# The low part of each MLP weight chunk: an accumulating DMA on a negated copy in place of a subtraction on DVE

## The reference, cut to what matters

```
h = rmsnorm(x, g)            # the first block adds shift and scale
y = square(relu(h @ W1)) @ W2    # W1: 1024 x 4096, W2: 4096 x 1024
x = x + y                    # the first block: x + gate * y
```

## Time and profile before

| | |
|---|---|
| time, median of 3 | 1957.42 us (1956.87 to 1958.24) |
| the profiled execution's own time | 1959.16 us |
| its span | 1957.3 us |
| PE busy | 1903.8 us |
| DVE busy | 966.7 us |
| ACT busy | 751.3 us |
| POOL busy | 76.7 us |
| matmuls | 8624 |

### The profile page before, as it was taken

The page is one execution under the profiler, slowest core; times in us unless marked ns, Lnnn a source line. Parts: engine busy times, 40 slices in busy tenths (PEclk is TensorE's granted clock), DMA queues, the critical chain, the costliest instruction groups (busy, mean ns, idle before and its releaser), DMA issues.

```text
span 1957.3 us, 21184 instructions
## 1 busy us (share of the span) xinstructions
PE 1903.8 (97%) x8624; PEld 1529.1 (78%) x8624; DVE 966.7 (49%) x1391; ACT 751.3 (38%) x1080; POOL 76.7 (4%) x94
## 2 busy tenths in 40 slices
PE   3999999989999999999999999999999999999999
PEld 2777668868888888877788888888877778888887
DVE  7367643554444346554554344445644554344443
ACT  4344443343323244356734232234445534233231
POOL 5100000010000000001100000000001000000000
PEclk9999999989999999999999999999999999999999
DMA  7445533313232223200122232322221122222222
GB/s 255 157 145 183 170 121 113 124 63 101 95 99 95 100 95 113 98 33 33 44 97 94 89 103 91 104 90 97 97 87 43 65 86 97 97 97 97 97 97 76
DMA packets 55121, 197.66 MB, mean 101 GB/s; under 512 B 6400, under 2 KB 6656, under 8 KB 55024
## 3 DMA queue, kind: packets, MB, share of 16 engines
q1 hardware_dynamic: 52272, 188.24, 28.2%
q0 software_dynamic: 2320, 7.31, 1.3%
q10 hardware_dynamic: 432, 0.74, 0.1%
HBM read 194.13 MB, written 2.14 MB: 100 GB/s over the span
## 4 chain that ended last, share of the span: by engine, by line
PE 93%; DVE 4%; ACT 2%; issue 0%; DMA 0%; POOL 0%; DVEq 0%; ACTq 0%
PE ps L252 26%; PE ps L254 25%; PE ps L253 25%; PE ps L288 2%; PE ps L290 2%; PE ps L289 2%; DVE RAW L1222 1%; PE ps L373 1%; PE ps L425 1%; PE ps L584 1%; PE ps L672 1%; DVE WL L1214 1%; PE ps L571 1%; PE ps L602 1%; PE ps L359 1%; PE ps L412 1%
## 5 line engine op out<-in xcount | busy, mean ns | idle before, releaser
L252 PE MATMUL ps<-R0h,WH 128*128 128x512 f32 x1200 | 471.6, 393 | 21.4 <-POOL R0l L1791 18.9
L1214 DVE TENSOR_TENSOR WL<-RAW,WH 128x1024 fp32r<-128x1024 f32 x303 | 372.3, 1233 | 241.0 <-ACT WH L769 237.5
L769 ACT ACTIVATE WH<-RAW 128x1024 fp32r<-128x1024 f32 x303 | 317.2, 1051 | 394.0 <-PE ps L254 339.5
L254 PE MATMUL ps<-R0h,WL 128*128 128x512 f32 x1200 | 468.2, 390 | 0.0
L253 PE MATMUL ps<-R0l,WH 128*128 128x512 f32 x1200 | 468.1, 390 | 0.0
L252 PE MATMUL ps<-R1h,WH 128*128 128x512 f32 x1064 | 420.8, 396 | 7.8 <-POOL R1l L1819 2.8
L253 PE MATMUL ps<-R1l,WH 128*128 128x512 f32 x1064 | 416.8, 392 | 0.0
L254 PE MATMUL ps<-R1h,WL 128*128 128x512 f32 x1064 | 416.7, 392 | 0.0
L252 PEld LDWEIGHTS ps<-R0h,WH 128*128 128x128 f32 x1200 | 225.9, 188 | 76.8 <-issue 16.5
L254 PEld LDWEIGHTS ps<-R0h,WL 128*128 128x128 f32 x1200 | 225.8, 188 | 47.4
L253 PEld LDWEIGHTS ps<-R0l,WH 128*128 128x128 f32 x1200 | 225.9, 188 | 46.1
(11 more groups left out here) (266 smaller groups left out, 1471.0 us busy)
## 6 DMA issues: line engine op xcount, KB each, us to landing
RAW<-in_W SPq DMA_DIRECT2D x351, 512.0 KB, 3.2
XT<-in_X SPq DMA_DIRECT2D x4, 512.0 KB, 7.7
ARENA<-bias_scratch POOLq DMA_DIRECT2D x8, 256.0 KB, 3.3
XT<-in_X POOLq DMA_DIRECT2D x8, 256.0 KB, 3.6
out_x<-XT SPq DMA_DIRECT2D x8, 256.0 KB, 2.0
ARENA<-bias_scratch POOLq DMA_DIRECT2D x8, 128.0 KB, 3.2
con<-in_CON POOLq DMA_DIRECT2D x1, 578.0 KB, 5.6
CSB<-in_CV ACTq DMA_DIRECT2D x1, 512.0 KB, 6.1
```

What stands on the lines that cost most here:

```text
L252: e.matmul(ps(b), wh, hi, start=first, stop=False)
L254: return e.matmul(ps(b), wl, hi, start=False, stop=last)
L769: e.activation(WH[:, n % NHL, :], RAW[:, i % NRAW, :], ACT.Copy).then_inc(sem["w_hi"])
L1214: e.tensor_tensor(WL[:, s, :], RAW[:, i % NRAW, :], r32(WH[:, s, :]), ALU.subtract).then_inc(sem["w_lo"])
```

## The change

For the 192 chunks of the three MLPs (`LATE_LO`), `WL` is no longer written by DVE. ACT, right after `WH`, writes a second rounded copy with the sign turned: `WL = -round(RAW)`, and signals `w_neg`. POOL waits for `w_neg` and starts a DMA that reads the chunk from DRAM once more and adds it to `WL` in place, so that `WL = W - round(W)`. TensorE waits for that DMA (`d_lo0` to `d_lo2`, one semaphore for each slot) in place of `w_lo`. SP frees a `RAW` tile on `w_neg` in place of `w_lo`. DVE skips these chunks. The other 111 split chunks stay as they were. POOL's waits and DMAs for all 64 chunks of an MLP stand in one run in its program (`weight_rests`): those of m0 behind the four low parts of the norm ahead of m0, those of m1 behind the heads' additions of the second block, those of m2 behind those of the third.

```diff
+LATE_LO = ("m0i", "m0o", "m1i", "m1o", "m2i", "m2o")
+BY_DMA = {key: n for n, key in enumerate(key for key in SPLITS if key[0] in LATE_LO)}
+BY_DVE = {key: n for n, key in enumerate(key for key in SPLITS if key[0] not in LATE_LO)}
+DMA_USE = {key: sum(NO[k] % NHL == NO[key] % NHL for k in BY_DMA if NO[k] <= NO[key]) for key in BY_DMA}
...
+                    elif before in BY_DMA:
+                        e.wait_ge(sem["w_neg"], BY_DMA[before] + 1)
                     else:
-                        e.wait_ge(sem["w_lo"], NO[before] + 1)
+                        e.wait_ge(sem["w_lo"], BY_DVE[before] + 1)
                 e.dma_start(RAW[:, r, :], W[i]).then_inc(sem[f"raw{r}"], 16)
...
+            def weights(key):
+
+                if key in BY_DMA:
+                    e.wait_ge(sem[f"d_lo{NO[key] % NHL}"], 16 * DMA_USE[key])
+                else:
+                    e.wait_ge(sem["w_lo"], BY_DVE[key] + 1)
...
                         if k == 0:
-                            e.wait_ge(sem["w_lo"], n + 1)
+                            weights(key)
                             open_bank(b)
...
                     e.activation(WH[:, n % NHL, :], RAW[:, i % NRAW, :], ACT.Copy).then_inc(sem["w_hi"])
+                    if SPLITS[n] in BY_DMA:
+                        e.activation(WL[:, n % NHL, :], RAW[:, i % NRAW, :], ACT.Copy,
+                                     scale=-1.0).then_inc(sem["w_neg"])
...
                 for n in itertools.islice(los, times):
+                    if SPLITS[n] in BY_DMA:
+                        continue
...
+            def weight_rests(tag):
+
+                for key in BY_DMA:
+                    if key[0][:2] == tag:
+                        s = NO[key] % NHL
+                        e.wait_ge(sem["w_neg"], BY_DMA[key] + 1)
+                        e.dma_start(WL[:, s, :], W[AT[key]], accum_op=ALU.add).then_inc(sem[f"d_lo{s}"], 16)
...
                 e.wait_ge(sem["h2_hi"], k + 1)
                 e.tensor_tensor(B[1][:, k, :], TMP[:, k % 4, :], r32(B[0][:, k, :]),
                                 ALU.subtract).then_inc(sem["h2_lop"])
+            weight_rests("m0")
             e.wait_ge(sem["mrg"], 24)
...
                 e.tensor_tensor(TS[:, 128:256], L[:, 1152:1280], TS[:, 256:384], ALU.add).then_inc(sem["ts"])
+            weight_rests("m1")
             e.wait_ge(sem["spv"], 8)
...
                 e.tensor_tensor(D[:, 256:384], D[:, 256:384], Wq[:, 1152:1280], ALU.add).then_inc(done)
+            weight_rests("m2")
```

More of the change, by code:

```diff
@@ L278, in vgemm_part @@
                 s = n % NHL
-                e.wait_ge(sem["w_lo"], n + 1)
+                weights((tag, c0 + c))
                 for tt, b in enumerate(banks):
@@ L467, in merge @@
                     s = i % NHL
-                    e.wait_ge(sem["w_lo"], i + 1)
+                    weights(("br", n))
                     for half in range(2):
```

## The result

The changed kernel takes 2073.38 us (2071.64 to 2076.81, 4 runs) against 1957.14 us (1956.81 to 1958.24, 4 runs) measured beside it: 116.2 us or 5.9% slower, ratio 1.0595 with a 95% interval of 1.0577 to 1.0613. The forecast was slower, 2015 us, +57.6 us. The time lies inside the range (1983 to 2115), but the loss is twice the one forecast.

The account below looks back on a forecast made before the run. TensorE's own pace bounds the MLPs, so only waits are added: m0's start 21.1 + 6.8, m1 and m2 16.2, i-phase stalls 11.6, m0's last o-phase 2.0, sum 57.7 on 1957.42: 2015 us. Range 1983 to 2115.

Parts of the forecast that it names:

- Rival 3: In the MLPs: matmuls start faster once DVE stops reading RAW and WH; 1952 us at 6.5 ns earlier each; chance 0.02.
- Rival 4: At the MLP starts: waits stay hidden, if POOL issues m0's DMAs before its norm work; 1957 us; chance 0.02.
- The slack: In the MLP chunks: time left for the DMA from issue to landing, 6.65 us in i-phases, 8.5 us in o-phases.
- D = 7.0: The accumulating DMA's time from issue to landing, taken as 7.0 us, between 6.0 and 8.6.
- the collision term: In the DMA's landing time: the RAW load, released by the same w_neg, shares the engines, adding up to 1.54 us.
- its table: Loss by other landing times: 4.5 us gives 25.5, 6.0 gives 38, 8.0 gives 98.7, 9.0 gives 157.7 us.
- rival 2: In all phases: the DMA is long, over 8 us, and becomes the bound; 2056 to 2115 us; chance 0.29.
- the likeliest band: A DMA landing time of 6 to 8 us, total time 1995 to 2056 us; chance 0.46.
- the 6.3 and 2.5 us: Start of m0: the second of three queued DMAs, issued at 430.24, lands 6.3 + 2.5 us later, at about 439.0.
- +215 at D = 10: Loss if the DMA's landing takes 10 us, by the same slopes, giving 2172 us; part of rival 2.
- half clock in m0's joint gemm: After the first wait in m0: 4.5 us at the 1.2 GHz level, 10 matmuls at twice 0.2267 us.
- The starts: First chunks of the MLPs: losses of 21.1 and 6.8 us at m0, 8.1 each at m1 and m2, together 16.2.

Follow-up runs that it names:

- the repaired kernels: Changed kernel with RAW load held until next chunk is rounded and each MLP's first five chunks on DVE; with negated copy before WH 1970.58 us, without 1971.21 us.

## Why the prediction was half right

**What bounds the kernel, and what the change could win: right.** PE's pace sets the MLPs; with all costs but ACT's copies taken out, the time is that of before (ratio 1.0003). Rival 3 (PE faster without DVE's reads) is refuted by the same run. Rival 4 (the starts hidden) fell in the changed kernel; its condition, POOL issuing m0's first DMAs earlier, takes 21 us off the first wait when it is met, and 14 us off the time.

**The slack: right within 0.2 us.** The stalls come at every third chunk that is split in an i-phase, where ACT's WH starts 2.1 us behind the next chunk, and but for one of 0.6 us there are none in the middle of o-phases. Only the last o-phase of m1 was wrongly taken for one with long slack; it lost 1.8 us here and 3.3 us with the W2 chunks alone by DMA. POOL's start behind ACT is 0.30 us, so the slack is 6.45 and not 6.65 us.

**The step that failed is D = 7.0, the size of the collision term.** With no RAW load near it the DMA took 5.6 us at the start of m0 (5.3 at the least of all 192), below the 6.0 that the prediction built from rows. To this it added about 1 us for the RAW load, and 1.54 at most, on the ground that a shared engine costs its own time. The runs show 7.8 with the load 0.3 us ahead and 5.9 with it 1.2 us ahead: 1.9 us, over the bound, while the load itself became 1.1 us slower. In the stall shown above the landing took 7.95 us, which is 7.95 - 6.45 = 1.5 us a stall instead of 0.35, or for 33 stalls 50 us instead of 11.6. So the mechanism was right and the size of one term wrong, and it weighed so much because D stood only 0.35 us above the slack.

That the time lies inside the range is in part luck. By the prediction's own steps the measured D of 7.8 gives about +90 us, and read at 8.0 its table gives +98.7; 116 us is what the table has for a D of about 8.3. The rest has other causes, of which these can be priced: POOL's 0.2 us more at 33 stalls (7 us), the clock (6 us) and the landings of 9.0 to 9.2 us at three fourth chunks (4 us); the rest is spread over the blocks. The time falls among those of rival 2 (D over 8, 2056 to 2115), but its condition was not met: D stayed in the likeliest band, and the o-phases did not stall.

Two smaller slips of the prediction: the 6.3 and 2.5 us by which it lets m0's second DMA land come from no row (measured: 7.45 us from issue to landing, 2.46 us behind the first), and its +215 at D = 10 uses the slope from 8 to 9, on which the o-phases stall for half of the way only; by its own steps it would be some 20 us more.

**The clock behind the fourth chunks was a smaller miss.** The prediction priced half clock in m0's joint gemm only and named as left out that of the short stalls. Those cost nothing: after waits of 1.2 to 1.5 us the clock stayed at 1.00. But the waits of 9.2 us at m0i 3 and of 4.4 and 4.6 us at the fourth chunks of m1 and m2 are followed by half clock: +2.4, +1.7 and +2.1 us in these chunks.

**The starts:** m0 up to chunk 3 came to 29.2 us for 27.9 forecast. Here two errors cancel: at the end of the joint gemm 20.1 us were lost for 21.1 forecast, at the fourth chunk another 9.1 for 6.8, as its DMA took 9.1 us and not 7.0. Those of m1 and m2 came to 13.3 and 15.3 for 8.1 each: longer landings (9.0 and 9.2 us at the fourth chunks), and the clock.

**Where it went, in sum:** 29.2 + 2.4 at m0, 28.6 at m1 and m2, 59.3 in the blocks, minus 2.0 between m0 and m1, plus 0.2 ahead of m0's norm: 117.7 by PE's timeline. Forecast, in the same order: 27.9, 0, 16.2, 13.6, 0.

The two pages cited: by the formula of the Trainium skill's page DMA: Bandwidth & Descriptors (Anatomy of one DMA) a POOL-queue transfer of 512 KB takes an estimated 3.2 us; that is under the 4.6 us measured for the plain copy with a load beside it and near the fastest of these, 3.4 us. The Trainium skill's page Collectives: The Full Stack (Why ReduceScatter is half of AllGather) has two source reads halve the rate, and the engine time agrees: 30.1% of 2074.9 us for the accumulates' queue against 15.3% of 1988.4 us with plain copies, twice as much.

What stays open: why sharing costs the DMA 1.9 us, more than the 1.54 us of engine time that the load takes, when the load becomes 1.1 us slower as well; what the landing would be with no load near it in steady use, which no run has; and why the landings of the repaired kernels scatter, which makes their last 10 us and was not tried further.

## What to carry to other kernels

Work moved off an engine that nobody waits for wins nothing, whatever its size; count first what the bounding engine waits for. A ring of slots turns the latency of each producer into a slack that can be read off a timeline; hold the new latency against it, and put into that latency what its own release starts at the same moment: here a load freed by the same semaphore cost more than the slack had left (1.9 us against 6.45 - 5.9), and one extra wait, which moved it by 4.5 us, took half of the loss away. In a queue run in program order, ask what stands ahead of the first item, not only how long each takes.

## What the runs showed of the hardware that was not expected

- An accumulating DMA of 128x1024 floats into SBUF: 5.3 us from issue to landing at best in the changed kernel (5.1 in other runs). Its median depends on when a 512 KB load of the other queue starts: 5.9 us when the load starts 1.2 us before it, 7.8 us when 0.3 us before it, 6.9 us when 0.7 us after it. The load beside it takes 3.5, 4.3 and 6.1 us then, and 3.2 us without such DMAs. With a second accumulating DMA 1.9 us behind it as well it took 9.0 to 9.2 us.
- A plain copy of the same size from the same queue: 3.4 us at best, 4.6 us beside the load. POOL's issue: 0.88 us for the accumulate, 0.53 for the copy.
- The 16 DMA engines were 0.86 busy over 250 us with stalls and 0.87 busy without: the share tells nothing of the waits.
- PE's granted clock fell to 0.50 within a wait of 9.2 us and around waits of 4.2 to 4.6 us (0.70 in the mean from 1100 to 1105 us), and stayed at 1.00 through waits of 1.2 to 1.5 us. Waits of 2.0 to 3.1 us in the other runs went both ways: half clock behind 3.09 us with the starts on DVE, full clock behind 2.97 us with the RAW load held.
